# Moving the new-key work and the first page step of paged decode attention into the last round of prompt attention

## The reference

```python
s = (einsum('bqhc,bkc->bhqk', q_lat, ckv) + einsum('bqhr,bkr->bhqk', q_pe, kpe)) * ATTN_SCALE
s = where(k_pos[None, :] <= q_pos[:, None], s, -inf)
p = softmax(s)
return einsum('bhqk,bkc->bqhc', p, ckv)
# new tokens: ckv = cache_mla_ckv[l][page_table] followed by the 8 new latents, kpe likewise
```

## Time and profile before

| | |
|---|---|
| median of 3 runs | 3527.52 us (3525.31 to 3530.98) |
| the profiled execution | 3525.47 us, span 3523.6 us |
| PE busy | 3387.0 us, 96% of the span |
| DVE busy | 1580.7 us, 45% |
| ACT busy | 964.4 us, 27% |
| POOL busy | 147.7 us, 4% |
| granted TensorE clock, mean | 0.978 of full speed |

### The profile page before, as it was taken

The page is one execution under the profiler, slowest core; times in us unless marked ns, Lnnn a source line. Parts: engine busy times, 40 slices in busy tenths (PEclk is TensorE's granted clock), DMA queues, the critical chain, the costliest instruction groups (busy, mean ns, idle before and its releaser), DMA issues. The chain is left out here.

```text
span 3523.6 us, 65059 instructions
## 1 busy us (share of the span) xinstructions
PE 3387.0 (96%) x28495; PEld 2193.9 (62%) x28495; DVE 1580.7 (45%) x2959; ACT 964.4 (27%) x2048; POOL 147.7 (4%) x175
## 2 busy tenths in 40 slices
PE   7999999999989999999989999999999999999998
PEld 5666655666656677765656666566665666776665
DVE  2211044555445788744322010544554467785522
ACT  3200123333245422211122000233332554222201
POOL 1000000000000022100000000000000001220000
PEclk8999999999999999999999999999999999999998
DMA  7112111211220277576011121111112204774521
GB/s 237 39 45 57 36 54 51 58 53 52 52 80 16 106 271 273 187 268 237 17 69 33 51 57 39 52 52 57 53 53 68 50 16 174 274 276 155 190 87 57
DMA packets 250912, 356.95 MB, mean 101 GB/s; under 512 B 47395, under 2 KB 222301, under 8 KB 242054
## 3 DMA queue, kind: packets, MB, share of 16 engines
q1 hardware_dynamic: 217590, 180.49, 17.0%
q0 software_dynamic: 16400, 155.53, 12.0%
q10 hardware_dynamic: 16640, 16.78, 1.5%
HBM read 302.17 MB, written 48.35 MB: 99 GB/s over the span
## 5 line engine op out<-in xcount | busy, mean ns | idle before, releaser
L958 PE MATMUL rwkv_gate_bank<-u,stream_ring 128*128 128x364 f32 (+1 forms) x2304 | 787.2, 482 | 2.0 <-PEq L869 2.0
L958 PEld LDWEIGHTS rwkv_gate_bank<-u,stream_ring 128*128 128x128 f32 x2304 | 413.0, 190 | 219.1 <-issue 8.5
L594 PE MATMUL mla_b<-u,stream_ring 128*128 128x364 f32 (+1 forms) x864 | 269.0, 474 | 15.6 <-PEq L2696 8.2
L594 PE MATMUL rwp_b<-u,stream_ring 128*128 128x364 f32 (+1 forms) x864 | 265.0, 468 | 2.8 <-PEq L777 2.8
L2335 PE MATMUL dec_s_bank<-u,att_q_rows 32*64 32x256 f32 x8192 | 242.9, 383 | 0.0
L594 PEld LDWEIGHTS mla_b<-u,stream_ring 128*128 128x128 f32 x864 | 165.9, 192 | 116.9 <-issue 20.2
L594 PE MATMUL conv_b<-u,stream_ring 128*128 128x364 f32 (+1 forms) x768 | 236.5, 469 | 0.0
L594 PEld LDWEIGHTS rwp_b<-u,stream_ring 128*128 128x128 f32 x864 | 163.5, 190 | 101.3 <-issue 3.9
L2722 PE MATMUL out_b<-merged,w_out 128*128 128x364 f32 (+1 forms) x672 | 214.5, 471 | 3.6 <-PEq L2598 3.6
L2335 PEld LDWEIGHTS dec_s_bank<-u,att_q_rows 32*64 32x64 f32 x8192 | 188.6, 134 | 35.8 <-issue 11.4
L594 PEld LDWEIGHTS conv_b<-u,stream_ring 128*128 128x128 f32 x768 | 145.1, 190 | 86.2
(11 more groups left out here) (537 smaller groups left out, 4580.1 us busy)
## 6 DMA issues: line engine op xcount, KB each, us to landing
stream_ring<-in_w_in_dram SPq DMA_DIRECT2D x100, 512.0 KB, 4.0
merge_sig<-gates_feature_major SPq DMA_DIRECT2D x16, 1632.0 KB, 9.4
gates_feature_major<-rwkv_gate_stage SPq DMA_DIRECT2D x96, 182.0 KB, 1.8
u<-in_w_ada_dram ACTq DMA_DIRECT2D x16, 1024.0 KB, 14.4
gates_feature_major<-rwkv_gate_stage SPq DMA_DIRECT2D x48, 180.0 KB, 2.0
w_out<-in_w_out_dram SPq DMA_DIRECT2D x14, 512.0 KB, 10.7
start_ada<-in_w_ada_dram SPq DMA_DIRECT2D x6, 1024.0 KB, 11.2
x_feature_major<-o_mla SPq DMA_DIRECT2D x2, 2176.0 KB, 9.4
```

The costliest lines, as they stand in the source:

```text
L594: mm = pe.matmul(self.banks[j % len(self.banks)][:, 0:m], self.stream.w(c, k), s.u[:, k, t0:t0 + m], start=(k == 0), stop=(k == KD - 1))
L958: mm = pe.matmul(self.banks[j % 2][:, 0:m], self.stream.w(self.first + n, k), self.s.u[:, k, t0:t0 + m], start=(k == 0), stop=(k == KD - 1))
```

## The change

Everything of the prologue is placed into round 3 of prompt attention or ahead of it, and the decode stage begins with the page loop itself.

- **Query rows.** `repeat` and its ACT copies are gone. SP issues 16 DMAs that copy `q_lat` into `q_rows`, 3 that copy the rotary queries to the other partition groups, and the load of the new latents, after the last piece of round 2.
- **New keys.** `new_scores` is a ring job at tile 7 of round 3, the turning of the new probabilities (`new_turn`) at tile 10, `new_values` two jobs at tile 11 and two at tile 12. DVE's softmax stands at tile 8, its sum at tile 10, ACT's exponential at tile 9.
- **Clearing and key turns on DVE.** The memsets stand at tile 2, page 0's key turns at tiles 6, 11 and 13.
- **Loads.** Page 1 is loaded during prompt attention. The decode stage begins with page 2; the rotary keys of page 2 and then pages 3 and 4 follow when the first step's scores are done.
- The rows of `s.u` that hold queries and keys of the two round parities change places, so that page 0's turned keys have a home that round 3 doesn't use.

```diff
+    new_at = {7: [(NP, "new_scores", 0)], 10: [(NP, "new_turn", 0)], 11: [(NP, "new_values", 0), (NP, "new_values", 1)],
+              12: [(NP, "new_values", 2), (NP, "new_values", 3)]}
...
-        pieces_at[a] = [(r + 1, *p) for p in pieces[first:first + after_tile.get(a % 16, 0)]] if r + 1 < NP else []
+        pieces_at[a] = [(r + 1, *p) for p in pieces[first:first + after_tile.get(a % 16, 0)]] if r + 1 < NP else new_at.get(a % 16, [])
...
+                sp.wait_ge(ring_read, slot[(NP - 1, "lat", 0)] + 1)
+                sp.dma_start(new_c, s.outs["ckv_sample"][l].rearrange("b t c -> t b c")).then_inc(new_in, 16)
+                for i in range(4):
+                    for j in range(4):
+                        sp.dma_start(q_rows[32 * j:32 * j + 32].rearrange("p (k i) b q -> p k i (b q)", i=4)[:, :, i, :],
+                                     q_lat[32 * i:32 * i + 32].rearrange("p k b h t -> p k (b h t)")).then_inc(rows_in, 16)
+                sp.wait_ge(q_pe_kept, 2 * NP)
+                for j in (0, 1, 3):
+                    sp.dma_start(q_pe[32 * j:32 * j + 32], q_pe[64:96]).then_inc(rows_in, 16)
+                sp.wait_ge(rows_in, 16 * 19)
...
+                    if what == "new_scores":
+                        pe.wait_ge(q_pe_kept, 2 * NP)
+                        pe.wait_ge(ring_read, slot[(NP - 1, "lat", 0)] + 1)
+                        for b in range(BATCHES):
...
+                    elif what == "new_values":
+                        pe.wait_ge(new_in, 16)
+                        pe.wait_ge(ring_read, slot[(NP, "new_turn", 0)] + 1)
...
+                pool.wait_ge(o_side_out, 16)
+                pool.wait_ge(rope_in[0], 128)
+                pool.wait_ge(rope_in[1], 128)
+                pages.load(pool, 1)
...
+                def beside(a):
+                    if a == 2:
+                        dve.memset(top_all[NQ:P, :], -1e30)
+                        dve.memset(total_all[NQ:P, :], 0.0)
+                        dve.memset(o_all[NQ:P], 0.0).then_inc(cleared, 1)
+                    elif a == 6:
+                        dve.wait_ge(scored, NEW)
+                        pages.turn_latent(dve, 0, 0)
+                    elif a == 8:
+                        new_softmax()
+                    elif a == 10:
+                        new_act.wait(dve, "exp")
+                        new_dve.done(dve.tensor_reduce(total_all[0:NQ, :], new_x[:], AX.X, ALU.add), "total")
+                    elif a == 11:
+                        pages.turn_latent(dve, 0, 1)
+                    elif a == 13:
+                        pages.turn_rotary(dve, 0)
...
             def _(pool):
-                for a in range(1, NS - 1):
+                pages.load(pool, pages.EARLY)
+                pool.wait_ge(scored, 8)
+                pages.load_rotary(pool, pages.EARLY)
+                for a in range(pages.EARLY + 1, NS):
                     pages.load(pool, a)
-                pool.wait_ge(repeated, 8)
-                new_pe.wait(pool, "scores")
-                pool.wait_ge(scored, 8)
-                for a in range(pages.EARLY, NS):
                     pages.load_rotary(pool, a)
-                pool.wait_ge(new_valued, 4)
-                pages.load(pool, NS - 1)
...
-                repeat(0)
-                new_scores(range(4))
-                repeat(1)
-                new_pe.done(new_scores(range(4, BATCHES)), "scores")
                 for a in range(G):
                     scores(a)
                     if a:
                         values(a - 1)
-                    else:
-                        new_values()
                     turn_probs(a)
...
+                dve.tensor_copy(top[:, :, 0], top_all[:]).then_inc(topped, 1)
+                dve.tensor_copy(total[:, :, 0], total_all[:]).then_inc(summed, 1)
+                pages.turn_latent(dve, 1, 0)
+                pages.turn_rotary(dve, 1)
                 for a in range(G):
                     maximum(a)
                     if a == 0:
+                        pages.turn_latent(dve, 1, 1)
```

More of the change, by code:

```diff
@@ L2088, in _ @@
                         exponential(a + 1)
+                    if a == NEW + 9:
+                        new_dve.wait(act, "shifted")
+                        new_act.done(act.activation(new_x[:], new_x[:], ACT.Exp, scale=ATTN_SCALE), "exp")
                     for p in pieces_at[a]:
@@ L2451, in _ @@
-                dve.memset(top[NQ:P, :, 0], -1e30).then_inc(cleared, 1)
-                dve.memset(total[NQ:P, :, 0], 0.0).then_inc(cleared, 1)
-                turn_keys(0)
-                new_pe.wait(dve, "scores")
-                new_dve.done(dve.tensor_tensor(x[:], latent[0:NQ, 0:BATCHES * STEPS].rearrange("p (b t) -> p b t", t=STEPS),
-                                               s.tab["new_keys"][0:NQ].unsqueeze(1).to_broadcast([NQ, BATCHES, STEPS]), ALU.add), "masked")
-                new_dve.wait(dve, "masked")
```

183 lines of the change are left out of this document (71 added, 112 removed).

## The result

The changed kernel takes 3533.2 us (median of 20 runs) beside 3526.65 us of the kernel before (20 runs on the same chip). The ratio is 1.0019, with a 95% interval from 1.0012 to 1.0025: it is slower, by about 6.5 us. I had forecast 3524, 3.6 us faster, so the sign is wrong; 3533.2 itself lies near the slow end of the stated range, 3513 to 3535. One of the 20 runs took 4991.86 us at a granted clock of 0.648 and is left out of the ratio, the other 19 lie between 3527.97 and 3543.77. In a later comparison on another chip (`after_again`, run 12) the ratio was 1.0025 (1.0016 to 1.0034).

A forecast was written before the change was run, and what follows sets the result against it. PE was taken to bound the page loop, at 8.70 us a step. Per layer, 15.7 gained - 11.4 paid in prompt attention - 2.5 for the clock = 1.8 us, 3.6 for both: forecast 3524 us, range 3513 to 3535.

The forecast's parts named there:

- The decode stage's start: Step 0 at E (last eviction's start) + 1.01, step 2 at E + 19.6 instead of 35.33: 15.7 us gained per layer.
- the fourth rival: Step 0's idle time brings 6.8 us of half clock over steps 0 and 1: 3526.5 us, chance 6%.
- I follow the seam up to there, since both kernels should be settled from that point on: Decode gain counted only to the old kernel's third-step scores, E + 35.33, against the new step 2 at E + 19.6.
- The memset stands at tile 2 where DVE is the bound and PE waits for it: 1.9 in full: Clearing at tile 2 of round 3 costs its own time, 1.9 us per layer.
- the 2.0 for the clock: Round 3: one clock fall after `new_scores`, about 6.80 us at half clock, costing 2.0 us per layer.
- small terms of 1.0: Round 3: 0.5 us for DVE's softmax and rotary turn, 0.5 for the ring waiting for ACT's copies, per layer.
- The half turns are covered: Page 0's 2.25 us half turns at tiles 6 and 11 cost nothing, hidden beside PE's `new_scores` and `new_values`.
- The pieces are paid in full: PE's moved `new_scores`, `new_turn` and `new_values` lengthen round 3 by their whole time, 8.5 us per layer.
- the second, two clock falls in round 3: Rival: `new_scores` and `new_values` each bring half clock, 17.0 us together; 3532 us, or 3536 without PE waits; chance 17%.

The follow-up runs named there:

- after_again: The unaltered changed kernel measured once more, on the chip also used for kernel 11: 3537.0 us, ratio 1.0025 to the kernel before.
- run 12: The same run as `after_again`, the unaltered changed kernel measured once more on another chip: 3537.0 us, ratio 1.0025 to the kernel before.
- run 5: Changed kernel with only page 5's load held until step 2's scores are done: 3532.3 us, ratio 1.0005.
- run 8: Changed kernel with the clearing behind tile 15's scaling, all of `new_values` in step 0 and page 5's load held: 3520.5 us, ratio 0.9969.
- kernel 11: The kernel of run 9 with page 0's half turns at tiles 12 and 14 instead of 6 and 11: 3519.1 us, ratio 0.9974.
- run 1: Changed kernel with the three memsets moved from tile 2 of round 3 to behind tile 15's scaling: 3530.3 us, ratio 1.0009.
- run 7: Changed kernel with page 0's half turns and rotary turn moved from round 3 back to the decode stage's start: 3542.5 us, ratio 1.0033.
- run 9: The kernel of run 8 with the latent half of `new_scores` spread over tiles 2 to 5 of round 3: 3510.5 us, ratio 0.9953.
- run 10: The kernel of run 1 with `new_scores` computed for only one of eight batches: 3525.1 us, ratio 0.9996.
- run 3: Changed kernel with half of `new_values` moved from tile 12 of round 3 into step 0's wait: 3526.8 us, ratio 0.9999.
- run 4: Changed kernel with pages 12, 17, 22 and 27 held in the settled loop, so two loads stand in a row: 3546.1 us, ratio 1.0056.

## Why the prediction was wrong

The terms of the sum, per layer. *The decode stage's start* was right as far as I followed it: E + 1.01, PE's wait of 3.02 us for the exponential (2.8), DVE's wait for page 2 (1.47 and 2.29 us, forecast 1.6 to 2.1), step 2 at E + 19.5 and 20.2 (19.6). Half clock did follow step 0's idle time, for 3.4 us from E + 8.8 in both layers, half as long as the fourth rival had it. Step 2 came on time in layer 0 all the same and 0.6 us late in layer 1, since the wait for page 2 stands behind it. The fit in "DMA: Bandwidth & Descriptors" of the Trainium skill, section "Anatomy of one DMA — SWDGE (gpsimd) path", gives an estimate of 6.8 us for page 2, by which it would have landed before DVE was free. DVE could start on it 1231.51 - 1223.05 = 8.5 us after its issue, so the row was the better guide.

**The first step that failed** is "I follow the seam up to there, since both kernels should be settled from that point on". The changed kernel is not settled at step 2: step 3 follows it by 12.81 and 10.19 us in the first profile and by 9.86 and 9.39 in `after_again`, not by 8.70. Pages 2 and 3 used to be loaded beside the slow prologue, and pages 4 and 5 apart, at E + 23.6 and 34.8. Now all four are issued from E + 2.2 to E + 18.9, beside the scores of steps 0 to 2, and PE stops among them. By step 2 the stage was 15.9 and 15.1 us ahead; step 2 then lost 4.1 and 1.5 to it and the later steps of layer 0 another 0.6, which leaves 11.2 and 13.7 at the last maximum. That a stop's place follows the page loads is what all profiles together show (run 5): held back, page 5 takes it from step 2 to step 4. How much time the hold saves they don't show. That late instructions are what stops PE is argued. In all 14 profiles PE stops 29 times for over 0.25 us inside a sequence of page matmuls with nothing awaited, and goes on 1.2 to 1.6 us behind the end of an instruction packet in 25 of them, though packets come only every 6 us or so. The other four (0.26 to 0.78 us, in step 1's scores of kernels 8 and 11) are 4.8 to 8.5 us behind one, and open. The packets themselves were not changed in any run.

**The second** is "The memset stands at tile 2 where DVE is the bound and PE waits for it: 1.9 in full". It cost 3.8 (run 1), since PE's wait brought a half-clock stretch that I had looked for only behind `new_scores` and in step 0.

The other terms of round 3: the tiles around `new_scores` are 5.8 us longer, for 4.3 and the 2.0 for the clock; those from `new_turn` on 5.5, for 4.2 with small terms of 1.0. With 3.8 for the clearing that is 15.1. *The half turns are covered* was right (run 7), and so was the reason: where the cover was taken away, 1.8 to 2.1 us per half turn came out (runs 9 and 10). *The pieces are paid in full* was right for a block at one tile and wrong as a rule: spread over tiles that DVE bounds, 2.4 us of PE work cost 0.5 (run 9).

Which of the two steps weighs more changes from profile to profile. Together: -15.1 + 11.2 = -3.9 in layer 0 and -15.1 + 13.7 = -1.4 in layer 1, 5.3 us slower, where 3.6 faster was forecast. Of the 8.9 between, 3.4 lie in round 3 and 5.5 in the decode stage (6.1 lost behind step 2, 0.6 won ahead of it). In `after_again` it is -17.7 + 12.9 and -17.8 + 14.6, 8.0 us slower, beside 8.8 measured; there 8.7 of the 11.6 between lie in round 3 and 2.9 in the decode stage. What the best kernel (run 9) regained on `after_again` lies in round 3 alone: 13.1 us per layer, while its last maximum is 0.4 to 1.3 us later.

The nearest rival was the second, two clock falls in round 3, with 3532. It had the number, but not the places: one fall came behind the clearing and one behind `new_scores`, none at `new_values`; by my estimate from the terms above they cost about 3.3 us per layer in the first profile and about 6 in `after_again`. In the first profile they would not have decided the sign without the 6.1 us lost behind step 2; in `after_again`, where 2.2 us were lost there, they would. So its 3532 is partly luck.

## What to carry to other kernels

- A settled loop's price holds once its transfers are settled too. When a change starts a loop earlier, lay out the queue of its prefetches again, and look for stops of PE where bulk loads follow each other without a pause. (That late instructions are the link is argued here, not shown.)
- Small work that is moved beside a pipeline is not priced by its own time alone: a wait of PE of 1.48 and 2.77 us in round 3 brought half clock behind it, and with that twice the price, while one of 0.75 us did not (run 9). Ask which engine bounds the tile it lands in; put DVE's work where DVE waits longest (the clearing: 3.8 us at tile 2, nothing at tile 15), and PE's in small parts where DVE bounds.
- The change was worth making with four corrections: clearing last, `new_values` in step 0's wait and page 5 held, `new_scores` spread. That kernel takes 0.9953 (0.9940 to 0.9967) of the time before, the change as it stood 1.0019. How much of it the hold of page 5 gave is not shown.

## What the hardware showed that I had not expected

- A queue of kind `instruction` brings 16 KB packets during the whole run, 64 bytes for each of PE's instructions, and counts on the same 16 DMA engines as the data. PE stopped for 0.3 to 2.0 us in the middle of a sequence and went on 1.2 to 1.6 us behind the end of such a packet. Most of these stops stand where the engines' share had been 0.9 to 1.0 for 10 us; five, of 0.28 to 1.19 us, stand in the settled loop of runs 3, 8, 9 and 10 at a share of 0.68 to 0.76, and one of 0.29 us in run 4 at 0.50.
- One program's half-clock stretches differ from run to run and layer to layer: 3.4 or 6.8 us behind the same instructions, so that round 3 took 58.3 or 60.9 us. This may be why the changed kernel's times scatter more (3528 to 3544 us in all but one of its 20 first runs, while most of before lie from 3525 to 3529).
- Filling an idle stretch of PE with matmuls of 8 rows did not keep the clock up: in run 8, half clock followed step 0 as before, for 3.4 us.
